# A conditioned decoder block on one core: the start of the kernel with inputs laid out by the host, the modulation columns summed on VectorE, and both halves' statistics ahead of them

## The reference, cut to what matters

```python
cond = jax.nn.silu(c)
mod = cond @ w_ada[l] + b_ada[l]                       # 9 * 1024 columns
sh1, sc1, gt1, sh2, sc2, gt2, sh3, sc3, gt3 = jnp.split(mod, N_MOD, axis=-1)
h = modulate(rms_norm(x, g_ffn1[l]), sh1, sc1)         # rms_norm(x) * g * (1 + sc1) + sh1
x = x + 0.5 * gt1[:, None, :] * swiglu(h, w1_a[l], w3_a[l], w2_a[l])
h = modulate(rms_norm(x, g_mix[l]), sh2, sc2)
x = x + gt2[:, None, :] * hybrid_mixer(h, w_in[l], ...)  # short convolution and state-space layer
h = modulate(rms_norm(x, g_ffn2[l]), sh3, sc3)
x = x + 0.5 * gt3[:, None, :] * swiglu(h, w1_b[l], w3_b[l], w2_b[l])
return rms_norm(x, g_final)
# swiglu(h, w1, w3, w2) = (silu(h @ w1) * (h @ w3)) @ w2
```

## Time and profile before

| | |
|---|---|
| three timed runs | 2112.83, 2113.22, 2114.67 us (median 2113.22) |
| the profiled execution | span 2111.0 us; the page gives no other time of its own |
| PE busy | 2066.9 us, 98% of the span |
| DVE / ACT / POOL busy | 65% / 35% / 67% |
| first 40 slices of 53 us | PE is under 90% busy only in the first and in the last |

### The profile page before, as it was taken

The page is one execution under the profiler, slowest core; times in us unless marked ns, Lnnn a source line. Parts: engine busy times, 40 slices in busy tenths (PEclk is TensorE's granted clock), DMA queues, the critical chain, the costliest instruction groups (busy, mean ns, idle before and its releaser), DMA issues.

```text
span 2111.0 us, 26148 instructions
## 1 busy us (share of the span) xinstructions
PE 2066.9 (98%) x9462; PEld 1695.1 (80%) x9462; DVE 1367.0 (65%) x1555; ACT 744.7 (35%) x1126; POOL 1405.3 (67%) x936
## 2 busy tenths in 40 slices
PE   7999999999999999999999999999999999999998
PEld 5778888888887778888888888887888888888887
DVE  6957868787778796877874654338537272635556
ACT  5633333333333453333333420116323333333334
POOL 1566878878785276856666655544858787778860
PEclk8999999999999999999999999999999999999999
DMA  8233251524232323233334444311111222111212
GB/s 301 60 115 105 67 174 41 155 85 120 90 110 65 123 83 96 80 107 97 91 93 153 161 158 147 110 50 40 53 47 41 60 61 60 50 51 50 70 42 80
DMA packets 220777, 197.41 MB, mean 94 GB/s; under 512 B 17028, under 2 KB 185136, under 8 KB 219504
## 3 DMA queue, kind: packets, MB, share of 16 engines
q1 hardware_dynamic: 196016, 154.42, 24.0%
q10 hardware_dynamic: 24640, 41.40, 6.0%
HBM read 169.45 MB, written 25.17 MB: 92 GB/s over the span
## 4 chain that ended last, share of the span: by engine, by line
PE 82%; DVE 8%; ACT 2%; issue 2%; DMA 2%; POOL 1%; ACTq 1%; SPq 0%; DVEq 0%; POOLq 0%
PE unit_d L1475 10%; PE unit_b L1475 10%; PE unit_b L1192 9%; PE unit_c L1475 7%; PE unit_a L1475 7%; PE unit_a L1192 6%; PE unit_a L1518 4%; PE unit_b L1518 4%; PE unit_b L1050 3%; PE unit_a L1050 2%; PE unit_d L1518 2%; PE unit_c L1518 2%; PE unit_d L1050 2%; PE unit_c L1050 2%; DMA ada_first<-in_w_ada 1%
## 5 line engine op out<-in xcount | busy, mean ns | idle before, releaser
L943 POOL TENSOR_TENSOR w_low<-raw,w_high 128x512 fp32r<-128x512 f32 x200 | 277.1, 1386 | 124.7 <-ACT w_high L1858 114.0
L1858 ACT ACTIVATE w_high<-raw 128x512 fp32r<-128x512 f32 x200 | 124.9, 630 | 294.2 <-PE unit_b L1475 117.7
L972 POOL TENSOR_TENSOR w_low<-raw,w_high 128x512 fp32r<-128x512 f32 x112 | 175.1, 1563 | 58.4 <-ACT w_high L1906 50.9
L894 POOL TENSOR_TENSOR w_low<-raw,w_high 128x512 fp32r<-128x512 f32 x80 | 119.1, 1488 | 111.1 <-ACT w_high L2068 107.2
L943 POOL TENSOR_TENSOR w_low<-w_mixed,w_high 128x512 fp32r<-128x512 f32 x76 | 105.5, 1388 | 37.7 <-ACT w_high L1858 33.5
L861 POOL TENSOR_TENSOR w_high<-raw,ones 128x512 fp32r<-128x512 f32 x44 | 59.4, 1349 | 98.1 <-PE unit_b L1050 33.4
L913 POOL TENSOR_TENSOR w_low<-raw,w_high 128x512 fp32r<-128x512 f32 x32 | 55.0, 1727 | 104.7 <-ACT w_high L1815 104.7
L2068 ACT ACTIVATE w_high<-raw 128x512 fp32r<-128x512 f32 x100 | 62.3, 630 | 163.2 <-PE unit_b L1192 108.2
L1906 ACT ACTIVATE w_high<-raw 128x512 fp32r<-128x512 f32 x112 | 67.8, 625 | 129.9 <-POOL raw L976 64.0
L1893 ACT ACTIVATE fg_high<-fg_two 128x1024 fp32r<-128x1024 f32 x56 | 59.4, 1061 | 145.8 <-PE unit_b L1518 45.7
L2763 DVE TENSOR_TENSOR fg_high<-fg_two,fg_high 128x1024 fp32r<-128x1024 f32 x56 | 95.7, 1710 | 0.0
(11 more groups left out here) (590 smaller groups left out, 6374.0 us busy)
## 6 DMA issues: line engine op xcount, KB each, us to landing
raw<-in_w_a SPq DMA_DIRECT2D x66, 512.0 KB, 4.4
raw<-in_w_b SPq DMA_DIRECT2D x66, 512.0 KB, 3.9
ada_ring<-in_w_ada SPq DMA_DIRECT2D x112, 256.0 KB, 3.0
raw<-in_w_in SPq DMA_DIRECT2D x44, 512.0 KB, 3.8
ada_first<-in_w_ada SPq DMA_DIRECT2D x8, 1024.0 KB, 20.6
sg_kept<-s ACTq DMA_DIRECT2D x16, 512.0 KB, 2.7
s<-sg_kept ACTq DMA_DIRECT2D x16, 512.0 KB, 3.3
x_rows<-in_x SPq DMA_DIRECT2D x8, 512.0 KB, 6.9
```

The lines of the kernel that those rows point to most:

```text
L894: pool.tensor_tensor(low_, mixer_plain(q, slots), high.bitcast(F32), ALU.subtract).then_inc(mixer.operand_low, 1)
L943: pool.tensor_tensor(low_, weight_plain(PRODUCTS[q][0], slots, mixed), high.bitcast(F32), ALU.subtract).then_inc(f.operand_low, 1)
L972: pool.tensor_tensor(low_, block_unit(here, u), high.bitcast(F32), ALU.subtract).then_inc(f.operand_low, 1)
L1858: act.activation(operand((here.ring[n] + q) % 4)[0], weight_plain(PRODUCTS[q][0], slots, mixed_of(here, n)), ACT.Copy).then_inc(f.operand_ ...
```

## The change

The host hands over most inputs in another layout: x by halves, with the channels of a tile on the partitions; w_ada with one output column to a partition and its 1024 inputs in a row; w1, w3 and w_in as whole 128-column tiles, contiguous; all small parameters as columns of one array `vt`. With this:

- The transposes of x and of the parameters go, with their copies. x is loaded straight into `x_res`, both halves ahead of everything else. ACT issues three loads in place of eleven.
- c comes as one row, PE spreads it over the partitions by two float32 matmuls (L1128 of the changed kernel), ACT makes silu of it in 128x1024 (`cond`).
- A modulation column is now one DVE instruction per column tile: it multiplies the tile of w_ada by `cond` and adds up along the row by its accumulator output (`accum_out`). There is no sum over the partitions on PE any more, for the first 16 tiles (`column_sum`, 128x1024 each) and for the other 56 (`ada_pieces`, in 14 windows of 8 pieces of 128x512, each piece half a row of a tile). For a window DVE first copies the half of `cond` to a free PSUM bank (`cond_copy`); from window 2 on it comes from DRAM, where ACT wrote it (`cond_kept`). PE's waits for `mod_added` become waits for `ada_used`.
- Windows 0 and 1 are both in matrix 1. Nothing stands between the activation sums of matrix 0 any more, and their order is t2, product of unit A and B, t1, t3, product of C and D, t4.
- The statistics of both halves come first (each sum in its own unit), then the 16 steps go by channel tile, both halves of a tile in turn, with the two column sums of the next tile between them. rstd lies in SBUF (`rstd_first`). All four first weight tiles are done together, step by step (`first_whole_tiles`): again 192 matmuls, but units A to D in each step. The second part of these tiles is split by ACT behind steps 2 and 3 of the channel loop, and POOL makes its low parts (`w_behind`).
- In the second FFN and the mixer only the layout of the loads changes.

The diff, cut to its core:

```diff
+B_ADA, GN, CW = 0, (NMOD, NMOD + KD, NMOD + 2 * KD), NMOD + 3 * KD
+DS = CW + 3 * KD
+GF = DS + NT
+AR = GF + KD
+VT = AR + 2 * KP
 PI = 3.141592653589793
...
+def window_columns(b):
+
+    return 2 * KD + KD * (0 if b < 2 else b - 1 if b < 8 else b - 7)
+
+
+def window_half(b):
+
+    return int(b == 1 or b >= 8)
+
+
+FIRST_STEPS = [(k, half) for k in range(KD) for half in range(2)]
...
+            def load_x(half):
+
+                for i in range(HK):
+                    sp.dma_start(x_res[:, 2 * i:2 * i + 2, HALF * half:HALF * half + HALF],
+                                 a["x"][half][:, 2 * i:2 * i + 2, :]).then_inc(x_loaded[HK * half + i], 16)
+
+            def load_pair(k):
+
+                if k >= RING_PAIRS:
+                    sp.wait_ge(ada_summed, 2 * (k - RING_PAIRS) + 2)
+                sp.dma_start(ada_pairs[k % RING_PAIRS][:, :, :],
+                             ada[0:2 * KD].rearrange("(s k) p n -> k p s n", s=2)[k]).then_inc(ada_loaded[k % RING_PAIRS], 16)
+
+            def load_part(z, part):
+
+                rows = slice(part * HK, part * HK + HK)
+                sp.dma_start(raw[:, z, rows, :], (tiles_1, tiles_3)[z % 2][z // 2][:, rows, :]).then_inc(
+                    (part_loaded[z], first_ffn.w_loaded[z])[part], 16)
+
+            load_x(0)
+            load_x(1)
+            load_pair(0)
+            load_part(0, 0)
+            load_part(1, 0)
+            load_part(2, 0)
+            load_part(3, 0)
+            load_pair(1)
+            load_pair(2)
+            for z in range(4):
+                load_part(z, 1)
+            for k in range(RING_PAIRS, KD):
+                load_pair(k)
...
                 for e in range(2):
                     load_matrix(here, 0, e)
                 if with_ada:
-                    sp.wait_ge(h_ready, 2 * KD)
+                    sp.wait_ge(rstd_ready, 2)
                     load_ada(0, 0, RING_ADA)
                 for e in range(2):
                     load_matrix(here, 1, e)
+                load_first_down()
                 if with_ada:
                     load_ada(0, RING_ADA, KD)
-                load_first_down()
-                if with_ada:
                     load_ada(1, 0, KD)
...
+            pe.wait_ge(c_row_loaded, 16)
+            for half in range(2):
+                last = pe.matmul(unit[A_][:, HALF * half:HALF * half + HALF], ones[0:1, :],
+                                 c_row[0:1, HALF * half:HALF * half + HALF], start=True, stop=True)
+            last.then_inc(setup_full, 1)
             for half in range(2):
                 for m in range(KD):
                     pe.wait_ge(sq_done, KD * half + m + 1)
-                    pe.matmul(unit[A_][:, HALF * half:HALF * half + HALF], ones[:, :], sq[:, m, :], start=(m == 0),
+                    pe.matmul(unit[(D_, C_)[half]][:, HALF:2 * HALF], ones[:, :], sq[:, m, :], start=(m == 0),
                               stop=(m == KD - 1)).then_inc(sq_used, 1)
 
             def statistics(n, half):
...
+            def first_whole_tiles(f):
+
+                pe.wait_ge(cond_ready, 1)
+                for n, (k, half) in enumerate(FIRST_STEPS):
+                    t = slice(HALF * half, HALF * half + HALF)
+                    xh, xl = (x[:, k % HK, :] for x in norm_operand(0, half, k // HK))
+                    pe.wait_ge(h_ready, n + 1)
+                    for u in range(4):
+                        if half == 0 and k % HK == 0:
+                            pe.wait_ge(f.operand_low, 4 * (k // HK) + u + 1)
+                        if n == 1 and u >= C_:
+                            pe.wait_ge(root_done, {D_: 1, C_: 2}[u])
+                        wh, wl = (x[:, k % HK, :] for x in first_operand(4 * (k // HK) + u))
+                        for part, (w, x) in enumerate(((wh, xh), (wh, xl), (wl, xh))):
+                            last = pe.matmul(unit[u][:, t], w, x, start=(k == 0 and part == 0),
+                                             stop=(k == KD - 1 and part == 2))
+                        if half == 1 and k % HK == HK - 1:
+                            last.then_inc(f.operand_used, 1)
...
-                    if n - 1 in here.mod_block and q == 2:
-                        pe.wait_ge(mod_added, here.mod_block[n - 1] + 1)
-                    if n in here.mod_block and q == N7 - 1:
-                        ada_tiles(here.mod_block[n])
...
+                    if f.n == 0 and here.first and n == 2 and q == 0:
+                        pe.wait_ge(ada_used, 2 * KD)
+                    if n - 1 in here.mod_block and q == 3:
+                        pe.wait_ge(ada_used, KD * (here.mod_block[n - 1] + 1))
...
+                squares(0, 0, KD)
+                root(0)
+                squares(1, 0, KD)
+                root(1)
+                own.then(act.activation(table[:, :], eps[:, :], ACT.Silu))
+                for o in range(2):
+                    whole_part_high(o)
+                act.wait_ge(vt_loaded, 16)
+                act.wait_ge(mod_done, 1)
+                factors(0)
+                step(0)
+                for o in (2, 3):
+                    whole_part_high(o)
+                step(1)
+                for k in range(1, KD):
+                    factors(k)
+                    step(2 * k)
+                    step(2 * k + 1)
+                    if k == 1:
+                        act.dma_start(cond_kept, cond[:, :]).then_inc(cond_kept_done, 16)
+                    if k in (2, 3):
+                        whole_part_high(2 * k)
+                        whole_part_high(2 * k + 1)
+
+            first_norm()
...
+                dve.wait_ge(cond_ready, 1)
+                first_root(0)
+                column_sum(0, 0)
+                column_sum(0, 1)
+                scaled(0)
+                first_root(1)
+                scaled(1)
+                low(0)
+                column_sum(1, 0)
+                low(1)
+                column_sum(1, 1)
+                for k in range(1, KD):
+                    scaled(2 * k)
+                    scaled(2 * k + 1)
+                    if k + 1 < KD:
+                        column_sum(k + 1, 0)
+                    low(2 * k)
+                    if k + 1 < KD:
+                        column_sum(k + 1, 1)
+                    low(2 * k + 1)
+                dve.wait_ge(h_ready, 2 * KD)
...
+            def cond_copy(b, free):
+
+                dve.wait_ge(*free)
+                if b >= 2:
+                    dve.wait_ge(cond_loaded, 16 * (b - 1))
+                from_ = cond[:, HALF * b:HALF * b + HALF] if b < 2 else cond_half[:, :]
+                dve.tensor_copy(cond_bank(b), from_).then_inc(cond_copied, 1)
+                dve.wait_ge(cond_copied, b + 1)
...
+                    dve.scalar_tensor_tensor(out=ada_ring[r][:, :], in0=ada_ring[r][:, :], scalar=1.0, in1=cond_bank(b),
+                                             op0=mul, op1=mul, accum_out=to).then_inc(ada_used, 1)
```

538 lines of the change are left out of this document (255 added, 283 removed).

## The result

The changed kernel takes 2121.64 us (median of 6 runs, 2119.86 to 2122.63) against 2113.27 for the kernel before (2112.82 to 2115.58): a ratio of 1.0038, 95% interval 1.0028 to 1.0049. I had forecast 2103.3, with a range of 2092 to 2120. Both the sign and the range were wrong.

What follows compares the result with a forecast made beforehand. PE, busy 98% of the 2111.0 us span, was taken as the bound. Terms -5.0 + 5.9 - 10.8 = -9.9 gave a span of 2101.1 and, with the median 2.2 above it, 2103.3 us; range 2092 to 2120.

Steps and rivals of the forecast that it cites:

- The way to the statistics: Kernel start: loads, silu and PE's sums of squares; second half's root at 28.1, PE's tile products from about 34.
- the first norm: DVE's channel steps and column sums after the statistics: ends at 79.2, 8.2 later than before.
- matrix 0: First chunk: PE waits until E+16.2, then runs cold; next matrix starts at E+35.7 = 114.9, 5.0 earlier.
- matrix 1: First chunk: sixteen column pieces on DVE make PE wait; matrix 2 starts 0.9 later than before.
- E: End of the first norm's last low part on DVE: forecast 79.2, before 70.98.
- the wait before tile 1: PE's wait in `first_down` for DVE's evacuation behind the column pieces: 5.9 us, plus 1.9 for cold matmuls.
- the six rounds: First norm on DVE: rounds of four products or low parts and two column sums, 6 x (2.4 + 2.8) = 31.2.
- The rival question, one pass or two: Whether a DVE column sum with accumulator passes once over its data (1.35, taken as 1.4) or twice (2.7).
- Rival A: First norm: column sums at half pace, 2.6 each, E at 95, time 2119; chance 0.17.
- The rest of the first FFN: From matrix 2 of chunk 1: twelve column sums dropped from PE, 0.2 plus eleven at 0.96, together -10.8.
- the slow clock: Cold PE after a wait: twelve matmuls take 5.4 in matrix 0; 1.9 charged at `first_down`'s wait.
- D: Rival: columns finish unhindered, but loads or waits elsewhere eat what PE drops; 2112, chance 0.05.

Runs made afterwards that it cites:

- e1: Kernel before, with PE's column sums left out for 12 of the 14 windows and nothing else changed; 2114.66 us, ratio 1.0004.
- e2: Changed kernel with twelve idle column sums (windows 2 to 13, results unused) put back on PE; 2116.95 us, ratio 1.0024.
- e4: Changed kernel with the fourth weight sum of each block down moved from GpSimd to DVE; 2115.61 us, ratio 1.0014.
- e7: Changed kernel with six pieces moved to matrix 0, e3's edit, later power tables, third and fourth down weight sums on DVE; 2096.84 us, ratio 0.9921.
- e9: e7's kernel with the 12 idle column sums of e2 put back on PE; 2106.16 us, ratio 0.9974.
- e3: Changed kernel, GpSimd's mixed sums written over the column ring only from matrix 3 of the last chunk, not matrix 2; 2114.59 us, ratio 1.0007.

## Why the prediction was wrong

**The way to the statistics, the first norm, matrix 0, matrix 1.** Right in its mechanisms and in its times: tile products from 34.9 (34), E 79.0 (79.2), matrix 1 at 114.0 (114.9), the wait before tile 1 5.4 (5.9), matrix 2 0.5 later than before (0.9, and one trace is good to 1 or 2 us there). That E is right to 0.2 is luck, for two terms were off and cancel. A column sum takes 1.22 us, and its reading of 0.08 overlaps with the next instruction: the next one starts 1.15 behind it, against my 1.4. That makes the six rounds 28.2 in place of 31.2. Beside GpSimd, DVE's operations lost 9.0 us (each one's time less that of the shortest of its form) where I had charged 6.4. The rival question, one pass or two, I had right: 1.19 ns a column with the accumulator, and 1.15 without it in the kernel before. The Trainium skill (Vector Engine (DVE) Microarchitecture Reference, "7. Points that are easy to get wrong") has such an instruction at half pace; this case's trace does not agree, by these two numbers.

**Rival A was near the time and has fallen.** It forecast 2119 and 2121.6 came, but its mechanism is not there: E is not at 95, and no column sum but two is beyond 2.1 us. A time that fits is no proof of a cause.

**The rest of the first FFN.** This is the step that failed: "The other eleven give 0.96 each: DVE's copy and accumulator I take as covered", -10.8 in all. In the matrices they did give it (9.9 in chunks 1 to 4). But I priced work that is dropped from PE at its full length because PE is busy 98% of the span, and asked only whether DVE's new work is covered. I did not ask who is ready just behind PE. Two places were:
- In each down of chunks 2 to 4 GpSimd's weight parts were ready only 0.2 to 0.5 us ahead of PE. PE comes 3 us earlier and GpSimd does not, so 9.9 us are lost again (10.4 with the 0.5 of chunk 1). Shown by e1 and e2 (removing 11.5 us of PE's work wins nothing, and adding it back costs nothing), e4 (with one of GpSimd's sums taken away the downs are 1.2 to 2.3 shorter) and e7 (with two, and the other reliefs, they are as short as before), e9 (then the work has its price).
- In the last chunk the power tables on DVE end just when PE needs the evacuation behind them. Here the changed kernel lost 9.5 where I had -0.96. Dropping the column sums alone brings 6.0 (e1), the rest of the change with PE's work put back brings 6.9 (e2), and e3 wins 6.1 back by not letting GpSimd wait for the ring. The shares overlap, since the length of the tables hangs on where GpSimd has its gap. Of the 9.5, 2.8 are the slow clock around the waits, a price that I had put on the waits ahead of chunk 1's second half and on none here.

The measured time of this step is +7.8 in place of -10.8. These 18.6 us are all but the whole error: 2121.6 is 18.3 above the 2103.3 of the forecast, and what is left over is the 0.4 at matrix 2 and a few tenths behind the first FFN.

**The chances.** I had given D, "loads or waits elsewhere eat what PE drops", 0.05 and a time of 2112. That was the right rival in kind (waits elsewhere), without a place or an engine, and even it stopped at eating up the gain. That a late engine behind PE can turn the sign, since one delay lengthens the next, I had not priced at all.
